# Seven block products for 7 of the 22 sets of the down projection, and the third sum of weights by accumulating DMA

## The reference

```
x = x + merged @ W_out
h = RMSNorm(x)
a = silu(h @ w_gate) * (h @ w_up)      # (256, 2048) @ (2048, 5632), twice
out = x + a @ w_down                   # (256, 5632) @ (5632, 2048)
```

## Time and profile before

| | |
|---|---|
| median of three runs | 2089.68 us (2089.66 to 2090.87) |
| profiled execution, its own time | 2089.39 us |
| its span, first to last instruction | 2087.7 us |
| PE busy | 2079.0 us |
| DVE busy | 1372.1 us |
| ACT busy | 1072.2 us |
| Pool busy | 144.5 us |
| DMA | 394.46 MB, mean 189 GB/s |

### The profile page before, as it was taken

The page is one execution under the profiler, slowest core; times in us unless marked ns, Lnnn a source line. Parts: engine busy times, 40 slices in busy tenths (PEclk is TensorE's granted clock), DMA queues, the critical chain, the costliest instruction groups (busy, mean ns, idle before and its releaser), DMA issues.

```text
span 2087.7 us, 28374 instructions
## 1 busy us (share of the span) xinstructions
PE 2079.0 (100%) x9658; PEld 1715.0 (82%) x9658; DVE 1372.1 (66%) x1677; ACT 1072.2 (51%) x1380; POOL 144.5 (7%) x174
## 2 busy tenths in 40 slices
PE   9999999999999999999999999999999999999999
PEld 7888877778888888888888888888888888888887
DVE  6676456665767777777664555577777887764443
ACT  5444455554566666666654444455555555543333
POOL 1121000000012222222000000000000000000000
PEclk9999999999999999999999999999999999999999
DMA  7656665554565555555575555556656666566554
GB/s 237 205 177 209 197 198 169 163 176 138 189 204 172 189 186 185 183 182 181 171 231 193 191 189 187 189 176 197 201 161 198 205 199 202 161 223 205 199 200 141
DMA packets 207541, 394.46 MB, mean 189 GB/s; under 512 B 15665, under 2 KB 21218, under 8 KB 207218
## 3 DMA queue, kind: packets, MB, share of 16 engines
q1 hardware_dynamic: 204530, 384.79, 56.7%
q0 software_dynamic: 2336, 8.46, 1.3%
q10 hardware_dynamic: 608, 0.34, 0.1%
HBM read 387.18 MB, written 2.16 MB: 186 GB/s over the span
## 4 chain that ended last, share of the span: by engine, by line
PE 93%; DVE 3%; issue 2%; DMA 1%; ACT 1%; DVEq 0%; SPq 0%; ACTq 0%
PE acc L1500 84%; PE side L1516 3%; PE side L1870 2%; DVE w_raw L1311 1%; PE side L1743 1%; DVE w_lo L1306 1%; PE acc L1870 1%; PE side L1598 1%; ACT w_hi L784 1%; DMA w_raw<-in_w_in 0%; DMA x_row<-in_x 0%; PE side L1749 0%; PE acc L1516 0%; PE side L1672 0%; DVE w_lo L847 0%
## 5 line engine op out<-in xcount | busy, mean ns | idle before, releaser
L847 DVE TENSOR_TENSOR w_lo<-w_raw,w_hi 128x1024 fp32r<-128x1024 f32 x536 | 668.2, 1257 | 538.0 <-ACT w_hi L463 537.1
L463 ACT ACTIVATE w_hi<-w_raw 128x1024 fp32r<-128x1024 f32 x536 | 564.0, 1058 | 708.0 <-PE acc L1500 651.9
L1500 PE MATMUL acc<-w_hi,h_hi 128*128 128x512 f32 x1280 | 511.4, 400 | 0.1
L1500 PE MATMUL acc<-w_hi,h_lo 128*128 128x512 f32 x1280 | 499.9, 391 | 0.0
L1500 PE MATMUL acc<-w_lo,h_hi 128*128 128x512 f32 x1280 | 498.8, 390 | 0.0
L784 ACT ACTIVATE w_hi<-w_raw 128x1024 fp32r<-128x1024 f32 x209 | 220.2, 1060 | 211.5 <-PE acc L1500 120.9
L1306 DVE TENSOR_TENSOR w_lo<-w_raw,w_hi 128x1024 fp32r<-128x1024 f32 x209 | 252.6, 1223 | 96.1 <-ACT w_hi L784 89.9
L1500 PEld LDWEIGHTS acc<-w_hi,h_hi 128*128 128x128 f32 x1280 | 240.7, 188 | 52.5 <-issue 5.5
L1500 PEld LDWEIGHTS acc<-w_hi,h_lo 128*128 128x128 f32 x1280 | 240.5, 188 | 51.5
L1500 PEld LDWEIGHTS acc<-w_lo,h_hi 128*128 128x128 f32 x1280 | 241.0, 188 | 49.3 <-issue 1.9
L1500 PE MATMUL acc<-w_hi,x2T_hi 128*128 128x512 f32 x528 | 206.7, 391 | 0.1
(11 more groups left out here) (276 smaller groups left out, 2352.2 us busy)
## 6 DMA issues: line engine op xcount, KB each, us to landing
w_raw<-in_w_in SPq DMA_DIRECT2D x320, 512.0 KB, 4.2
w_raw<-in_w_ffn_gate SPq DMA_DIRECT2D x88, 512.0 KB, 3.7
w_raw<-in_w_ffn_up SPq DMA_DIRECT2D x88, 512.0 KB, 4.5
w_raw<-in_w_ffn_down SPq DMA_DIRECT2D x88, 512.0 KB, 3.5
w_raw<-in_w_ssm_proj SPq DMA_DIRECT2D x64, 512.0 KB, 4.2
w_raw<-in_w_attn_proj SPq DMA_DIRECT2D x32, 512.0 KB, 3.5
w_raw<-in_w_out SPq DMA_DIRECT2D x32, 512.0 KB, 3.5
acs_b<-acs_scratch POOLq DMA_DIRECT2D x16, 512.0 KB, 7.1
```

Of the source, the lines that this page charges most:

```text
L463: nc.scalar.activation(w_hi[:, r], w_raw[:, r], ACT.Copy).then_inc(hi_ready, 1)
L847: nc.vector.tensor_tensor(w_lo[:, r], w_raw[:, r], w_hi[:, r].bitcast(F32), ALU.subtract).then_inc(lo_ready, 1)
L1500: done = nc.tensor.matmul(acc[p][:, t], a[:, k0 + kk, cut], w[:, r, kk], start=first and kk == n == 0, stop=last and kk == UK - 1 and n == 2)
```

## The change

The down projection takes its chunks in pairs, as the FFN takes gate and up: columns 0 and 1, then 2 and 3. A pair has 11 sets of four units, in an order of their own (`DOWN_ORDER`), and 3 of the first pair's and 4 of the second's (`DOWN_SEVENS`) are done with seven products. The four sums of the stationary side are kept for each of the four groups of k tiles concerned (`down_s_hi`, `down_s_lo`), made in plain sets (`down_sums`). P1, P5, P6 and P7 add up in `side` over the sets of a pair, and DVE adds their combinations to `x2` (`combined`) before the output rows are made. The third sum of weights, B12+B22, is no longer made by DVE but by a DMA that Pool issues, from slot 2 into slot 1 with addition, in the 11 iterations of the FFN and in the 7 sets of the down projection. DVE waits for it before the next sum. In the FFN Pool runs a small operation on two columns ahead of each of these DMAs. The stores of the first two chunks come in the second pair, that of the third after all loads.

```diff
+DOWN_SETS = KF // (2 * UK)
+DOWN_ORDER = ((0, 1, 3, 5, 2, 7, 4, 8, 6, 9, 10), (0, 2, 1, 4, 3, 6, 5, 8, 7, 9, 10))
+DOWN_SEVENS = ((2, 4, 6), (2, 4, 6, 8))
+DOWN = [(g, s, n) for g in range(2) for s in DOWN_ORDER[g] for n in range(len(PRODUCTS) if s in DOWN_SEVENS[g] else 4)]
+FIRST_DOWN = 4 * DOWN_SETS + 3 * len(DOWN_SEVENS[0])
+SEVENTH = [(g, s) for g in range(2) for s in DOWN_ORDER[g] if s in DOWN_SEVENS[g]]
+PLAIN_UNITS = UPC * (7 * D // CW + 2 * G) + 3 * UPC * D // CW
...
-            for c in range(D // CW):
-                for u in range(KF // UK):
-                    load(w_ffn_down, u * UK, c * CW)
-                    if c and u == KF // UK // 2:
-                        store(c - 1)
+            for g in range(2):
+                for position, s in enumerate(DOWN_ORDER[g]):
+                    first, second = 2 * UK * s, 2 * UK * s + UK
+                    one, other = 2 * g * CW, 2 * g * CW + CW
+                    if s in DOWN_SEVENS[g]:
+                        for row, col in ((first, one), (first, other), (second, other), (second, one)):
+                            load(w_ffn_down, row, col)
+                        unit.n += OPERANDS - RAWS
+                    else:
+                        for row, col in ((first, one), (second, one), (first, other), (second, other)):
+                            load(w_ffn_down, row, col)
+                    if g and position in (3, 5):
+                        store((position - 3) // 2)
+            store(2)
...
+                    elif n == 4:
+                        act.wait_ge(third_summed, i * 16 + 16)
                     else:
-                        act.wait_ge(weights_summed, i * 4 + (n - 2))
+                        act.wait_ge(weights_summed, i * 3 + (1, 0, 2, 3)[n - 3])
...
+            def down_hi(n):
+                g, s, m = DOWN[n]
+                loads = 4 * (g * DOWN_SETS + DOWN_ORDER[g].index(s))
+                source = m
+                if s in DOWN_SEVENS[g]:
+                    nth = FF // CW + SEVENTH.index((g, s))
+                    source = RAW_SLOT[m]
+                    if m == 4:
+                        act.wait_ge(third_summed, 16 * nth + 16)
+                    if m in (3, 5, 6):
+                        act.wait_ge(weights_summed, 3 * nth + (1, 0, 2, 3)[m - 3])
+                act.wait_ge(raw_in[source], (raw.n + loads) * (16 // RING) + 16)
+                act.wait_ge(mm_done, unit.now(1 - RING))
+                nc.scalar.activation(w_hi[:, unit.slot % RING], w_raw[:, source], ACT.Copy).then_inc(hi_ready, 1)
+                unit.step()
+            def down_sums_hi(j):
+                act.wait_ge(s_summed, j + 2)
+                nc.scalar.activation(down_s_hi[:, j], down_s_sum[:], ACT.Copy).then_inc(s_hi_ready, 1)
+            for n in range(LEAD, len(DOWN)):
+                down_hi(n)
+                g, s, m = DOWN[n]
+                if n == 6:
                     product_hi(FF // CW - 1)
+                if (g, s, m) in ((0, 1, 1), (0, 3, 1), (0, 5, 1), (1, 0, 1)):
+                    down_sums_hi(((0, 1), (0, 3), (0, 5), (1, 0)).index((g, s)))
+                if s == DOWN_SEVENS[g][-1] and m == len(PRODUCTS) - 1:
+                    act.wait_ge(mm_done, unit.now(-LEAD))
+                    act.wait_ge(s_lo_ready, 4 + g)
+                    nc.scalar.activation(p1_row[:], side[:, 2], ACT.Copy).then_inc(p1_ready, 1)
...
-                        weights_sum(1, 1, 2)
-                        dve.wait_ge(weights_summed, i * 4 + 2)
+                        dve.wait_ge(third_summed, i * 16 + 16)
                         weights_sum(2, 0, 2)
                     if at == FIRST7 - LEAD + 3:
-                        dve.wait_ge(weights_summed, i * 4 + 3)
+                        dve.wait_ge(weights_summed, i * 3 + 2)
...
+            def down_lo(n):
+                g, s, m = DOWN[n]
+                source = RAW_SLOT[m] if s in DOWN_SEVENS[g] else m
+                r = unit.slot % RING
+                dve.wait_ge(hi_ready, unit.now(1))
+                nc.vector.tensor_tensor(w_lo[:, r], w_raw[:, source], w_hi[:, r].bitcast(F32), ALU.subtract).then_inc(lo_ready, 1)
+                unit.step()
+            def down_sums(j):
+                s = DOWN_SEVENS[1][j]
+                dve.wait_ge(a_lo_ready, s + 1)
+                k = 2 * UK * s
+                link(nc.vector.tensor_tensor(down_h_sum[:], a_hi[:, k:k + 2 * UK].bitcast(F32), a_lo[:, k:k + 2 * UK].bitcast(F32), ALU.add))
+                a11, a21, a12, a22 = (down_h_sum[:, UK * n:UK * (n + 1), P * t:P * (t + 1)] for n in range(2) for t in range(TT))
+                nc.vector.tensor_tensor(down_s_sum[:, S3], a11, a21, ALU.subtract)
+                link(nc.vector.tensor_tensor(down_s_sum[:, S1], a21, a22, ALU.subtract))
+                link(nc.vector.tensor_tensor(down_s_sum[:, S2], a11, down_s_sum[:, S1], ALU.subtract))
+                nc.vector.tensor_tensor(down_s_sum[:, S4], a12, down_s_sum[:, S2], ALU.subtract).then_inc(s_summed, 1)
+            def down_sums_lo(j):
+                dve.wait_ge(s_hi_ready, j + 2)
+                nc.vector.tensor_tensor(down_s_lo[:, j], down_s_sum[:], down_s_hi[:, j].bitcast(F32), ALU.subtract).then_inc(s_lo_ready, 1)
+                dve.wait_ge(s_lo_ready, j + 2)
...
+            def combined(g, part):
+                one, other = (slice((2 * g + p) * CW, (2 * g + p + 1) * CW) for p in range(2))
+                if part == 0:
+                    dve.wait_ge(mm_done, unit.now(-LEAD))
+                    dve.wait_ge(p1_ready, FF // CW + g + 1)
+                    link(nc.vector.tensor_tensor(v_sum[:], side[:, 1], p1_row[:], ALU.subtract))
+                    link(nc.vector.tensor_tensor(y_sums[:], v_sum[:], side[:, 3], ALU.subtract))
+                if part == 1:
+                    nc.vector.tensor_tensor(v_sum[:], side[:, 0], v_sum[:], ALU.add)
+                    link(nc.vector.tensor_tensor(p5_sum[:], side[:, 0], y_sums[:], ALU.add))
+                    nc.vector.sem_inc(mids_free, 1)
+                if part == 2:
+                    nc.vector.tensor_tensor(x2[:, 0, one], x2[:, 0, one], p1_row[:], ALU.add)
+                    link(nc.vector.tensor_tensor(x2[:, 1, one], x2[:, 1, one], y_sums[:], ALU.subtract))
+                if part == 3:
+                    nc.vector.tensor_tensor(x2[:, 0, other], x2[:, 0, other], v_sum[:], ALU.add)
+                    link(nc.vector.tensor_tensor(x2[:, 1, other], x2[:, 1, other], p5_sum[:], ALU.add))
...
+            for n in range(LEAD, len(DOWN)):
+                down_lo(n)
+                g, s, m = DOWN[n]
+                nth = FF // CW + (SEVENTH.index((g, s)) if s in DOWN_SEVENS[g] else 0)
+                if s in DOWN_SEVENS[g] and m == 0:
+                    dve.wait_ge(raw_in[1], (raw.n + 4 * (g * DOWN_SETS + DOWN_ORDER[g].index(s))) * (16 // RING) + 16)
+                    weights_sum(0, 0, 1)
+                if s in DOWN_SEVENS[g] and m == 2:
+                    dve.wait_ge(third_summed, 16 * nth + 16)
+                    weights_sum(2, 0, 2)
+                if s in DOWN_SEVENS[g] and m == 3:
+                    dve.wait_ge(weights_summed, 3 * nth + 2)
+                    weights_sum(3, 2, 3)
+                if n == 7:
+                    product_lo(FF // CW - 1)
+                for j, (first, last) in enumerate((((0, 1, 0), (0, 1, 2)), ((0, 3, 0), (0, 3, 2)), ((0, 5, 0), (0, 5, 2)),
+                                                   ((1, 0, 0), (1, 0, 2)))):
+                    if (g, s, m) == first:
+                        down_sums(j)
+                    if (g, s, m) == last:
+                        down_sums_lo(j)
+                if s == (9, 7)[g] and m == 3:
+                    combined(g, 0)
+                if s == (10, 9)[g] and m < 3:
+                    combined(g, m + 1)
+                if n - LEAD in (FIRST_DOWN - 3, FIRST_DOWN - 1):
+                    out_rows((n - LEAD - FIRST_DOWN + 3) // 2)
+            dve.wait_ge(mm_done, unit.now(-2))
+            cut = slice(2 * CW, 3 * CW)
+            dve.wait_ge(out_done[0], 16 * TT)
+            for t in range(TT):
+                nc.vector.tensor_tensor(out_row[:, 0, t], acc[0][:, t], x2[:, t, cut], ALU.add).then_inc(out_ready, 1)
+            c = D // CW - 1
+            dve.wait_ge(out_done[1], 16 * TT)
+            dve.wait_ge(early_rows, 1)
+            for first, last in ((0, 0), (0, CW // 2), (CW // 2, CW)):
+                t = 1 if last else 0
+                if last == CW // 2:
+                    dve.wait_ge(mm_done, unit.now(0))
+                part = slice(first, last if t else CW)
+                nc.vector.tensor_tensor(out_row[:, 1, t, part], acc[1][:, t, part],
+                                        x2[:, t, c * CW + first:c * CW + (last if t else CW)], ALU.add).then_inc(out_ready, 1)
...
+            def third_weights_sum(i):
+                pool.wait_ge(pool_step, own.now())
+                pool.wait_ge(weights_summed, i * 3 + 1)
```

(77 more changed lines are left out.)

15 lines of the change are left out of this document (5 added, 10 removed).

## The result

The changed kernel takes 2103.03 us (median of 4 runs, 2100.4 to 2103.98), the kernel before 2089.67 us beside it: 1.0062 times as long, with a 95% interval of 1.0045 to 1.008. It is slower by 13.4 us, where 2076.8 us was forecast, and lies 1 us above the range. The profiled run, the shortest of the four, took 2100.4 us (span 2098.7); before it was 2089.39 (2087.7).

The account below looks back on a forecast made before the run. PE was taken as the bound (busy 2079.0 of 2087.7 us): 2089.39 - 9.52 (matmuls) - 3.6 (FFN) + 0.3 (end) = 2076.6 us, 2076.8 by the median; range 2074.5 to 2102 us.

Parts of the forecast that it names:

- The fewer matmuls: Down projection: each of 7 converted sets needs 42 matmuls instead of 48, saving 1.36 us each, 9.52 us in all.
- Both fit, so I price them at nothing: Second pair: added DVE work (16.0 us) and ACT work (11.7 us) fit in PE's 20.40 us, so cost zero.
- Loads behind the set lose nothing by a late DMA: Slot 0 is refilled after w_lo of P5; that and PE shift together, so no added loss.
- a few stalls in the alternating sets where loads overlap the DMA: Rival of a partly late DMA: up to 9 us given back, 2077 to 2086 us; chance 0.17.
- The sums of the stationary operands: Four times in down-projection plain sets, 2.86 us of DVE plus low and high parts; cost zero, uncertainty 0.4 us.
- its tightest place: First set of the second pair, where out_rows(0) comes behind the stationary sums too: 0.4 us left before PE waits.
- The landing of the accumulating DMA: Issue to landing of the third sum's DMA: 4.8 us estimated, against a limit of 4.95 us.
- that number decides all: Sign to check: whether the accumulating DMA lands below 5 us from its issue was to decide the outcome.
- The FFN's gain: Third sum by DMA ends PE's wait for w_lo at P7: 0.33 us in each of 11 iterations, 3.6 us.
- The tail: End of kernel: two 256 KB stores run into the last ones, adding 0.3 us (0 to 1).
- the slow accumulation: Rival, both stages: DMA slower than its window; at 6.05 us, 18 sets lose 1.1 us each, 2096.6 us; chance 0.23.
- the descriptors held back: Rival: DMA descriptors go out only after DVE's w_lo of P2, landing in 6.6 us; 2106 us; chance 0.07.

Follow-up runs that it names:

- half loads: Changed kernel with every down-projection load bringing only the first of two k tiles (256 KB, not 512 KB; wrong weights): 2079.32 us, ratio .9953.
- P2 late: Changed kernel with P2 behind P3 and P5 in down-projection converted sets, third sum there by DVE: 2096.68 us; with two plain sets between, 2084.11 us.
- FFN alone: Kernel before, with only the FFN's third sum of weights made by the accumulating DMA that Pool issues: 2087.43 us, ratio .999.
- plain copy: Changed kernel with a copy of slot 2 over slot 1 in place of the accumulating DMA, both stages (third sum wrong): 2094.42 us, ratio 1.0027.
- two or three plain sets between: Changed kernel with converted down-projection sets further apart: six with two plain sets between, 2088.45 us; four with three between, 2085.52 us.

## Why the prediction was wrong, point by point

**The fewer matmuls** were right: 42 x 0.2267 = 9.52 us. The kernel with half loads lets them be seen, 8.1 us of them.

**"Both fit, so I price them at nothing"** is the step that failed, with its companion **"Loads behind the set lose nothing by a late DMA"**. I summed the work of DVE (16.0 us) and ACT (11.7 us) against PE's 20.40 us and called w_lo's lead of four units the cover. I did not sum the third resource, the four raw slots. In a plain set a slot is held for a load, a w_hi and a w_lo. In a converted set slots are also held for sums, a second use and a DMA, and all four are then given back within 4.5 us (1981.56 to 1986.10 in SP's queue). The sum could have been made from rows shown: 5.78 us of DVE (five operations at about 1.14), two loads at 3.4, 2.3 for the plain unit, 0.5 for Pool and my 4.8 for the DMA are 20.2 us of 20.40 for slot 2. For slot 3 the same rows give 1.1 us of w_hi, eight operations of DVE from the w_lo of P2 on (9.1), 2.3 and two loads, 19.3 us. That leaves next to no cover, and the loads asked for in a burst took 4.4 to 6.3 us instead of 3.4. The measured cycle of slot 2 is 25.3 us, and that of slot 3 ends within 0.35 us of it. Cost: some 22 us where I had put 0. The rival "a few stalls in the alternating sets where loads overlap the DMA" named the place, but priced it at 9 us at most, counted it as still faster, and put it on the DMA, for which DVE waited only 2.8 us.

The Trainium skill (Perfetto Trace Analysis, Optimization Strategy) says that the same gap, repeated on the engine that should be saturated, can mean that SBUF lacks room for the next tile. The chain and the half loads agree with it: the gaps return with the converted sets and all but go away when a slot is refilled faster. They shrink as well when the same slots are used in another order (P2 late).

**The sums of the stationary operands** were priced at 0 with 0.4 us of doubt; without them the kernel is 3 to 5 us faster. 1.1 us of it is where the prediction saw its tightest place, PE waiting for `out_rows` (the weight load's wait on DVEq L1468, at 1966.95). The rest shares the stalls of the sets beside them and was not separated.

**The landing of the accumulating DMA** was right: estimate 4.8, measured 4.5 (11 in the FFN 4.5 to 4.6; in the down projection up to 6.0, where loads run beside it). But "that number decides all" was not: it was below 5 us, and the kernel was slower. (The limit of 4.95 us is 4.97 by the two times that it is taken from.)

**The FFN's gain** had the right mechanism and a wrong size: 3.6 us forecast, 1.7 measured alone. ACT's writes of a_hi in the changed kernel, to compare with the earlier trace rows:

```profile
1595.88 1.01 ACT L789 ACTIVATE a_hi<-side 128x1024 f32 x1
...
1639.03 1.00 ACT L789 ACTIVATE a_hi<-side 128x1024 f32 x1
```

43.15 us, where 43.1 was forecast and 43.41 was before. From the first such write (1423.11) to the tenth (1812.33) it is 389.2 us; before 391.6, and 388.6 in the FFN alone. That is 2.3 and 3.0 us in 9 iterations, 0.26 to 0.33 each, close to the 0.33 forecast. The head's iteration gives back 1.7 us (from P1's first weight load, 1387.36, to a_hi's write 35.75 us; before 34.06). With the plain copy it is 33.6 us, so the late DMA is the cause. Pool in the head's iteration of the changed kernel, and DVE and PE behind it:

```profile
1382.83 0.48 POOL L1542 TENSOR_TENSOR small<-small,pool_constants 128x2 f32<-128x2 f32 x1 [355.81 <-ACT x_sq L825]
...
1384.32 0.94 POOL L1624 TENSOR_TENSOR small<-small 128x2 f32<-128x2 f32 x1
1385.21 0.95 POOL L1626 DMA_DIRECT2D w_raw<-w_raw  x1
```

```profile
1389.85 1.23 DVE L1368 TENSOR_TENSOR w_raw<-w_raw 128x1024 f32<-128x1024 f32 x1 [2.42 <-DMA w_raw<-w_raw]
```

```profile
1392.27 0.19 PEld L2021 LDWEIGHTS side<-w_hi,s_hi 128*128 128x128 f32 x1 [0.87 <-DVE w_lo L1363]
1394.54 0.19 PEld L2021 LDWEIGHTS side<-w_hi,s_hi 128*128 128x128 f32 x1 [1.05 <-DVE w_lo L1363]
```

The first sum was done at 1383.3 us, but Pool was still at the reciprocal root of the norm, so the DMA was issued at 1385.21, 1.95 us after the sum; in the iteration at 1600 us it was 0.6. DVE lost 2.42 us and PE 0.87 + 1.05 us. I had multiplied one iteration by 11 and not asked what stood in Pool's queue in the first. How much of the gain is left is uncertain: the traces of the kernels with this same FFN have 461.9 to 464.1 us for it, against 464.0 in the one trace before.

**The tail:** 3.2 us, as before; 0.3 forecast. **The rivals:** the slow accumulation and the descriptors held back fall with the landing of 4.5 us. The rule of the Trainium skill (SBUF — State Buffer, Summary: rules for kernel authors) is that descriptors are starved while DVE is in a 2x or 4x perf mode; nothing of the kind shows here beside w_lo, a tensor_tensor in fp32: the DMA issued at 1601.69, with a w_lo from 1601.94 to 1603.17, landed in 4.6 us, and the one issued at 1998.44, with DVE idle until 2001.79, took 6.04.

**What stays open:** how the 22 us divide between order, burst and DMA, since the edits to the down projection alone gave from 1 us (the plain copy, in that stage) to 24 us (half loads) and they overlap; and why with two or three plain sets between (with the DMA) PE still waits right behind a converted set. That it is the four loads asked for together is argued from their landings (medians of 5.0 and 4.8 us), not shown apart, and loads of half the bytes do not tell a burst from loads that are slow for another reason. Also, loads land in 4.3 to 4.5 us in the two kernels without any converted set in the down projection, 3.5 before; no run says why, and PE does not wait for them.

## What to carry to other kernels

Beside each engine's work per period, add up the cycle of each buffer: load, every operation until it is given back, and the next load, at the landing time of a burst. An order of work that fits on every engine can still make the engine that is the limit wait, if it holds buffers longer. Do the sum for every buffer of a ring: where two cycles are nearly as long, shortening one step of one of them gains little, as the plain copy shows. And price the first iteration of a loop by itself when a step moves to a queue that does something else there.

## What the runs showed of the hardware

An accumulating DMA of 512 KB from SBUF to SBUF landed 4.5 us after its issue with nothing beside it and kept Pool for 0.86 us (down projection); the same DMA as a plain copy landed after 2.9 us and kept it for 0.53. The Trainium skill (DMA: Bandwidth & Descriptors, Anatomy of one DMA — SWDGE (gpsimd) path) gives 2.0 us and the bytes at 436 GB/s, an estimate of 3.2 us for one stream of 512 KB and of 4.4 us for two. The accumulation fits two streams; the copy is a little faster than its rule.

Stalls have a second price. After PE had stood still for 2.7 us, its granted clock fell to 0.50, the 1.2 GHz level (starts, lengths; then the window with busy time of five engines, clock, DMA share, GB/s):

```profile
2003.07 0.79 PE L2021 MATMUL acc<-w_hi,a_hi 128*128 128x512 f32 x1 [2.51 <-DVE w_lo L1439]
2003.67 0.63 PE L2021 MATMUL acc<-w_lo,a_hi 128*128 128x512 f32 x1
2004.09 0.63 PE L2021 MATMUL acc<-w_hi,a_lo 128*128 128x512 f32 x1
```

```profile
2003.00:2006.00 3.00, 2.93 (x7) 2.35 (x8) 2.65 (x4) 1.71 (x2) 0.00 (x0) 0.50 0.07 12
```

The first start is followed after 0.59 us, and the next six come 0.38 to 0.43 us apart instead of 0.2267, 1.2 us more. It happened once in this trace; the shorter gaps (up to 1.8 us between starts) were followed by one start at 0.34 us each. In the other runs gaps of 2.0 to 2.5 us left the pace as it was, but for one of 2.5 in the kernel without stationary sums, after which the starts were 0.43 us apart again.
